# One transformer layer with an expert mixture: gate products of 256 columns in two parts, and 36 early expert blocks

## What is computed

```python
eid = jnp.take_along_axis(cand_i, pos, axis=-1)     # expert number: row * 128 + column
gate = jax.nn.softmax(top_s, axis=-1)
a = jnp.einsum('td,tkd->tk', hb, peer_u[eb], preferred_element_type=jnp.float32)
a = jax.nn.gelu(a, approximate=False)
return jnp.einsum('tk,tkd->td', (gb * a).astype(hb.dtype), peer_v[eb])
```

## Time and profile before

| | |
|---|---|
| median of the runs | 980.63 us (979.21 to 981.70) |
| the profiled execution | 980.77 us, span 979.0 us |
| TensorE busy | 962.2 us, 98% of the span |
| VectorE, ScalarE, GpSimd busy | 749.8, 464.6, 189.0 us |
| granted TensorE clock | 1.00 |
| gate stage, first to last product of L1788 | 246.3 to 324.4 us |
| moved | 172.57 MB |

### The profile page before, as it was taken

One profiled execution on the slowest core, in us unless ns is written; L12 is line 12 of the kernel. 1 busy time (PEld: TensorE's weight loads), 2 busy tenths in 40 slices (PEclk: granted clock), 3 DMA queues, 4 the chain that ended last, 5 costly groups with the idle time before them and its releaser, 6 DMA issues.

```text
span 979.0 us, 16833 instructions
## 1 busy us (share of the span) xinstructions
PE 962.2 (98%) x5606; PEld 845.1 (86%) x5606; DVE 749.8 (77%) x1385; ACT 464.6 (47%) x715; POOL 189.0 (19%) x232
## 2 busy tenths in 40 slices
PE   7999999999999999999999999999999999999998
PEld 7998899998999888888888888888888888888887
DVE  5899767988999887777777777777777777777776
ACT  5566544432777534444444444444444443444442
POOL 3064227986887100000000000000000000000000
PEclk9999999999999999999999999999999999999999
DMA  8633129845222676555555545555555555555554
GB/s 247 189 118 130 56 86 331 211 110 150 82 76 66 212 239 227 173 201 184 187 198 178 208 173 201 184 189 196 177 209 173 203 181 192 193 182 204 173 205 158
DMA packets 70164, 172.57 MB, mean 176 GB/s; under 512 B 6752, under 2 KB 35552, under 8 KB 69616
## 3 DMA queue, kind: packets, MB, share of 16 engines
q1 hardware_dynamic: 68080, 167.47, 50.7%
q0 software_dynamic: 576, 4.19, 2.1%
q10 hardware_dynamic: 1472, 0.44, 0.2%
HBM read 163.16 MB, written 4.72 MB: 171 GB/s over the span
## 4 chain that ended last, share of the span: by engine, by line
PE 75%; DVE 1%; issue 0%; POOL 0%; DVEq 0%
PE psum L1849 36%; PE psum L1829 20%; PE psum L1832 10%; PE psum L1788 6%; PE psum L1795 2%; PE psum L1715 1%; DVE big L1127 0%; PE psum L1478 0%; DVE big L1271 0%; DVE big L1138 0%; PE psum L1776 0%; DVE big L1173 0%; POOL big L1374 0%; DVE big L1169 0%; DVE big L1158 0%
## 5 line engine op out<-in xcount | busy, mean ns | idle before, releaser
L1849 PE MATMUL psum<-rr 128*128 128x512 f32 x1536 | 368.8, 391 | 0.0
L1849 PEld LDWEIGHTS psum<-rr 128*128 128x128 f32 x1536 | 287.9, 188 | 58.8
L1829 PE MATMUL psum<-h_all,rr 128*128 128x512 f32 x856 | 306.7, 392 | 0.0
L755 ACT ACTIVATE rr<-raw 128x1024 fp32r<-128x1024 f32 x109 | 115.6, 1060 | 274.5 <-PE psum L1849 274.5
L1193 DVE TENSOR_TENSOR rr<-raw,rr 128x1024 fp32r<-128x1024 f32 x109 | 133.6, 1225 | 145.6 <-ACT rr L755 145.6
L1832 PE MATMUL psum<-h_all,rr 128*128 128x256 f32 x856 | 221.9, 280 | 0.0
L1829 PEld LDWEIGHTS psum<-h_all,rr 128*128 128x128 f32 x856 | 160.6, 188 | 32.2 <-DVE rr L1132 0.6
L1832 PEld LDWEIGHTS psum<-h_all,rr 128*128 128x128 f32 x856 | 160.8, 188 | 8.3
L641 ACT ACTIVATE rr<-raw 128x1024 fp32r<-128x1024 f32 x107 | 113.6, 1061 | 61.9 <-DMA raw<-in_peer_u_dram 60.5
L1132 DVE TENSOR_TENSOR rr<-raw,rr 128x1024 fp32r<-128x1024 f32 x107 | 130.6, 1220 | 3.5 <-ACT rr L641 1.7
L1179 DVE TENSOR_TENSOR rr<-psum,picks 128x2048 fp32r<-128x2048 f32 x32 | 72.1, 2287 | 8.3 <-PE psum L1788 6.6
(11 more groups left out here) (202 smaller groups left out, 945.5 us busy)
## 6 DMA issues: line engine op xcount, KB each, us to landing
raw<-in_peer_u_dram SPq DMA_DIRECT2D x128, 512.0 KB, 4.0
raw<-in_peer_v_dram SPq DMA_DIRECT2D x128, 512.0 KB, 3.5
big<-in_w_in_dram SPq DMA_DIRECT2D x10, 1024.0 KB, 5.9
big<-in_peer_wq_dram SPq DMA_DIRECT2D x8, 1024.0 KB, 6.2
big<-in_w_out_dram SPq DMA_DIRECT2D x4, 1024.0 KB, 5.2
rr<-big POOLq DMA_DIRECT2D x4, 1024.0 KB, 8.6
up_kept<-gel SPq DMA_DIRECT2D x20, 128.0 KB, 3.6
gel<-up_kept SPq DMA_DIRECT2D x20, 128.0 KB, 3.5
```

The source lines that it names most:

```text
L755: act.activation(v_sp[s][:, 0, :], v_raw[s], ACT.Copy).then_inc(v_hi, 1)
L1829: return pe.matmul(both, ut[s][:, 0, k, :], ht[:, :, k, :], start=(k == 0), stop=(k == DK - 1))
L1849: i = pe.matmul(psum[:, 4 + 2 * t + n, :], g_sp[:, s, x, t * P:(t + 1) * P], v_sp[s][:, y, n * 512:(n + 1) * 512], start=(first and m == 0 ...
```

## The change

- A weight is kept as a high part (fp32r, in the buffer `hm`) and a low part (`picks[:, 2]`). The scaled columns of a token become 2 x 128 columns, one-hot x high and one-hot x low (`pairs_at`), fp32r. One fp32r product of 256 columns a token takes the place of the native one of 128 columns.
- A group's products go in two halves of four tokens, each into two PSUM banks. ScalarE copies the high half into `gates` (`keep_high`), VectorE adds the low half from PSUM (`add_low`).
- VectorE compares rows as before (1024 elements, iota in PSUM), and columns in bfloat16 with all operands in SBUF (`iota16`, `col16`), laid out [column][token], so that a token's columns lie 16 bytes apart. ScalarE scales three tokens of a group (six instructions of 128), GpSimd five (two of 640).
- 36 early blocks instead of 20, all native. TensorE's parts of blocks 13 to 35 are spread over the groups (`fill`): 12 parts ahead of the first group, 6 after the last, the other 166 between. They use the PSUM banks 0, 6 and 7 in turn. The Gelu of a block stands two groups behind its last part.
- `t32s` gets an SBUF buffer of its own, and so do the up weights of block 36 (`u_first`), which are loaded and split ahead of the gate stage.
- The values of blocks 0 and 1 are loaded while the last early blocks run, 2 and 3 after the last columns are scaled. `RING_END` is 31.

```diff
-NQ, OHS = SEQ // GRP, 3
-EARLY, EARLY_TOP = 20, 14
-RING_END = 19
-ACT_T = 2
+NQ, RS = SEQ // GRP, 3
+HALF = GRP // 2
+EARLY, EARLY_TOP = 36, 14
+RING_END = 31
+ACT_T = 3
+FILL0 = EARLY_TOP - 1
+PRE, TAIL = 12, 6
+def fill_end(q):
+    between = DK * (EARLY - FILL0) - PRE - TAIL
+    return PRE + (0 if q < 0 else between * (q + 1) // (NQ - 1) if q < NQ - 1 else between + TAIL)
+def filled_after(e):
+    return next(q for q in range(-1, NQ) if fill_end(q) >= DK * (e - FILL0 + 1))
...
+        cols = raw[:, 2 * D:3 * D].bitcast(BF16).rearrange("p (s n q) -> p s q n", s=2, q=GRP)
+        rows_at = [rr[:, n:n + D].rearrange("p (q n) -> p q n", q=GRP) for n in (2 * D, 3 * D, 6 * D)]
+        pairs_at = [rr[:, n:n + 2 * D].rearrange("p (q a n) -> p q a n", q=GRP, a=2) for n in (7 * D, 4 * D)]
+        def half_sums(c, part):
+            return psum[:, 2 + 2 * (c % 2):4 + 2 * (c % 2), :].rearrange("p b (q a n) -> p a n (b q)", q=2, a=2)[:, part]
         def early_bank(e):
-            return (2, 5)[e % 2] if e < EARLY_TOP - 1 else 0
+            return (2, 5)[e % 2] if e < FILL0 else (0, 6, 7)[(e - FILL0) % 3]
...
             def keep_early(e):
                 sp.wait_ge(e_up, e + 1)
-                if e + 3 < EARLY_TOP:
+                if e + 3 < EARLY:
                     load_ring(e + 3)
-                elif e < EARLY_TOP and e % 3 < 2:
-                    load_u(U_FIRST[e % 3])
-                elif e == EARLY - 1:
+                elif e == EARLY - 3:
                     sp.dma_start(v_first, pv[0]).then_inc(ld_vf, 16)
-                elif e >= EARLY_TOP:
-                    load_u(e + 2)
+                elif e == EARLY - 2:
+                    load_v(1)
+                if e == FILL0 - 4:
+                    sp.dma_start(u_first.rearrange("p k n -> p (k n)"), pu[EARLY]).then_inc(ld_uf, 16)
...
-            for b in range(1, 3):
-                sp.wait_ge(b_done, NQ - 3 + b)
+            sp.wait_ge(ohg_up, NQ)
+            sp.wait_ge(ohp_up, NQ)
+            for b in range(2, 4):
                 load_v(b)
...
-            act.activation(iota_in, iota, ACT.Copy).then_inc(a_iota, 1)
+            act.activation(iota_in, iota, ACT.Copy)
+            act.activation(iota16, iota.unsqueeze(2).to_broadcast([P, NK, GRP]), ACT.Copy).then_inc(a_iota, 1)
+            act.wait_ge(ld_uf, 16)
+            act.activation(ut[0][:, 0], u_first, ACT.Copy).then_inc(ut_hi, 1)
             act.wait_ge(d_sub, 1)
...
+            def gated(q, first, last):
+                for j in range(first, last):
+                    tok = GRP * q + j
+                    for part, scale in ((0, f(p_hi(tok, 1))), (1, picks[:, 2, tok:tok + 1])):
...
+                        i = act.activation(pairs_at[q % 2][:, j, part, :], cols[:, q % 2, j, :], ACT.Copy, scale=scale)
...
+            def keep_high(c):
+                act.wait_ge(b_done, c + 1)
+                act.activation(gates[:, :, HALF * c:HALF * c + HALF], half_sums(c, 0), ACT.Copy).then_inc(b_ev, 1)
             for q in range(NQ):
+                act.wait_ge(oh_up, 2 * q + 2)
+                if q >= 2:
+                    act.wait_ge(b_done, 2 * q - 2)
+                gated(q, 0, 1)
                 if q:
+                    keep_high(2 * q - 2)
+                    keep_high(2 * q - 1)
+                gated(q, 1, ACT_T)
+                for e in range(FILL0, EARLY):
+                    if filled_after(e) + 2 == q:
+                        early_gelu(e)
...
+            keep_high(2 * NQ - 2)
+            keep_high(2 * NQ - 1)
+            for e in range(FILL0, EARLY):
+                if filled_after(e) + 2 >= NQ:
+                    early_gelu(e)
...
+            def add_low(c):
+                dve.wait_ge(b_ev, c + 1)
+                mine = gates[:, :, HALF * c:HALF * c + HALF]
+                dve.tensor_tensor(mine, half_sums(c, 1), mine, ALU.add).then_inc(g_add, 1)
+            dve.wait_ge(ut_hi, 1)
+            dve.tensor_tensor(ut[0][:, 1], u_first, f(ut[0][:, 0]), ALU.subtract).then_inc(ut_lo, 1)
             for q in range(NQ):
+                if q >= RS:
+                    dve.wait_ge(b_done, 2 * (q - RS + 1))
+                ones(rows_at[q % RS], 0, GRP * q, GRP)
...
+                if q >= 2:
+                    add_low(2 * q - 4)
+                    add_low(2 * q - 3)
+                    dve.wait_ge(ohg_up, q - 1)
+                    dve.wait_ge(ohp_up, q - 1)
+                dve.tensor_tensor(cols[:, q % 2].rearrange("p q n -> p n q"), iota16, col16[:, GRP * q:GRP * q + GRP].unsqueeze(1).to_broadcast([P, NK, GRP]),
+                                  ALU.is_equal).then_inc(oh_up, 1)
...
+            def gated(q):
+                n, tok = GRP - ACT_T, GRP * q + ACT_T
+                for part, p in ((0, f(p_hi(tok, n))), (1, picks[:, 2, tok:tok + n])):
...
+                    i = pool.tensor_tensor(pairs_at[q % 2][:, ACT_T:, part, :], cols[:, q % 2, ACT_T:, :],
+                                           p.unsqueeze(2).to_broadcast([P, n, NK]), ALU.mult)
+                i.then_inc(ohp_up, 1)
             for q in range(NQ):
+                pool.wait_ge(oh_up, 2 * q + 2)
+                if q >= 2:
+                    pool.wait_ge(b_done, 2 * q - 2)
+                gated(q)
...
             def early_ready(e):
+                if e >= FILL0 + 3:
+                    pe.wait_ge(e_gel, e - 2)
...
+            def gate_half(q, h):
+                c = 2 * q + h
+                if c >= 2:
+                    pe.wait_ge(g_add, c - 1)
+                for j in range(HALF):
+                    i = pe.matmul(psum[:, 2 + 2 * (c % 2) + j // 2, (j % 2) * SEQ:(j % 2 + 1) * SEQ], rows_at[q % RS][:, HALF * h + j, :],
+                                  pairs_at[q % 2][:, HALF * h + j].rearrange("p a n -> p (a n)"), start=True, stop=True)
+                i.then_inc(b_done, 1)
...
+            early_part(EARLY_TOP - 2, DK // 2, DK).then_inc(e_up, 1)
+            fill(0, fill_end(-1))
+            pe.wait_ge(e_gel, EARLY_TOP - 1)
+            for q in range(NQ):
+                pe.wait_ge(ohg_up, q + 1)
+                pe.wait_ge(ohp_up, q + 1)
+                gate_half(q, 0)
+                gate_half(q, 1)
+                fill(fill_end(q - 1), fill_end(q))
...
+            pe.wait_ge(e_gel, EARLY - (EARLY - 1 - FILL0) % 3)
+            first_up(0, EARLY)
+            pe.wait_ge(g_add, 2 * NQ)
+            pe.wait_ge(e_gel, EARLY)
```

More of the change, by code:

```diff
@@ L118, in layer @@
         gel = sb("gel", [P, 2, SEQ])
+        t32s = sb("t32s", [P, DK, SEQ])[:, :, :]
+        u_first = sb("u_first", [P, DK, P])[:, :, :]
         psum = ctx.enter_context(nc.psum_tensor("psum", [P, 8, 512], F32))
@@ L212, in layer @@
         u_raw = raw[:, 0:2 * D].rearrange("p (s k n) -> p s k n", s=2, k=DK)
-        u_ring = [raw[:, n:n + D] for n in (0, D, 4 * D)]
+        u_ring = [raw[:, n:n + D] for n in ((D, 4 * D, 0)[(e - EARLY) % 3] for e in range(3))]
         v_raw = [raw[:, 2 * D:3 * D], raw[:, 4 * D:5 * D]]
@@ L706, in _ @@
             early_gelu(EARLY_TOP - 2)
[L708 to L716, removed]
-            act.wait_ge(pk_ev, 2)
@@ L720, in early_hi @@
[L720 to L727, removed]
-            for q in range(NQ):
[L730 to L737, removed]
-                if q:
[L739 to L749, removed]
@@ new lines, in gated @@
+            def gated(q, first, last):
+                for j in range(first, last):
+                    tok = GRP * q + j
+                    for part, scale in ((0, f(p_hi(tok, 1))), (1, picks[:, 2, tok:tok + 1])):
+                        if tok == 0 and part:
+                            act.wait_ge(d_plo, 1)
+                        i = act.activation(pairs_at[q % 2][:, j, part, :], cols[:, q % 2, j, :], ACT.Copy, scale=scale)
+                if last == ACT_T:
+                    i.then_inc(ohg_up, 1)
@@ new lines, in fill @@
+            def fill(first, last):
+                for n in range(first, last):
+                    e, k = FILL0 + n // DK, n % DK
+                    if k == 0:
+                        early_ready(e)
+                    i = early_part(e, k, k + 1)
+                    if k == DK - 1:
+                        i.then_inc(e_up, 1)
+            early_part(EARLY_TOP - 2, DK // 2, DK).then_inc(e_up, 1)
+            fill(0, fill_end(-1))
+            pe.wait_ge(e_gel, EARLY_TOP - 1)
+            for q in range(NQ):
@@ L1783, in gate_group @@
                 pe.wait_ge(ohg_up, q + 1)
                 pe.wait_ge(ohp_up, q + 1)
-                if not first:
-                    pe.wait_ge(b_ev, q - OHS + 1)
-                for j in range(GRP):
-                    i = pe.matmul(psum[:, 2 + 2 * s + j // 4, (j % 4) * P:(j % 4 + 1) * P], f(oh[:, s, 0, j, :]), oh_g[:, s, j, :],
-                                  start=True, stop=True)
-                i.then_inc(b_done, 1)
-            def split_part(e, first, last):
-                for k in range(first, last):
```

(4 more changed lines are left out.)

92 lines of the change are left out of this document (29 added, 63 removed).

## The result

The changed kernel takes 983.00 us (980.75 to 983.96), the kernel before in the same comparison 980.75 (978.90 to 981.98): a ratio of 1.0026, 95% interval 1.0016 to 1.0035. So the forecast gain of 11 us is not there. The kernel stands 2.3 us above the one before: the interval leaves out 1, but that is less than the 2.9 us that the prediction took as the least it could tell. The profiled execution took 983.88 us, its span 982.1.

The account below looks back on a forecast made before the run. TensorE was taken to bound the kernel nearly everywhere. 980.8 - 11.9 (TensorE net) + 0.3 (start) + 0.5 (downs) = 969.7 us against the profiled execution, 969.5 against the median; range 965 to 990.

Parts of the forecast that it names:

- The pace of the stage: Gate stage: TensorE slowest at 3.26 us a group, against VectorE 3.1, ScalarE 3.0 and GpSimd up to 3.2.
- I take no surcharge: Gate stage: ScalarE's and GpSimd's reads of 16-bit columns at a 16-byte step were charged nothing extra.
- A row that speaks against the change: Passage on strided column reads: VectorE's L1127 at 64 bytes needs 1.90 ns an element, against 1.18 for neighbours.
- the 0.72 that I had as the upper end: Gate stage: highest surcharge considered for the 16-byte step, in ns an element, from VectorE's strided row.
- Rival 1: Gate stage: ScalarE sets the pace, deciding from 0.345 us a copy; 973 to 981 us, chance 0.25.
- rival 2: Gate stage: GpSimd sets the pace, products 1.59 us, round 3.87; 989 us, slower than before, chance 0.2.
- the lead of 0.2 us of TensorE: Gate stage: TensorE at 3.26 us a group is slowest by 0.2, a narrow lead and most of the risk.
- The lock: Gate stage: VectorE's column comparison, both operands in SBUF, holds GpSimd up, making its round 3.2 us.
- TensorE's prices: TensorE: native part 0.432 us, gate product 0.1185, late block's up product 2.77; net change -11.9 us.
- The wait ahead of the first down product: After the gate stage: store and load, 3.6 us each, leave TensorE idle 4.1 us; ends nothing and 4.5.
- The start and the downs: Ahead of the gate stage, u_first's load and copy add 0.3 us; late value loads in down blocks add 0.5.
- the half microsecond of cover: Before the gate stage: about half a microsecond spare around u_first's copy; without it up to 0.7 us more.

Follow-up runs that it names:

- the first two runs: Changed kernel with neighbouring elements in place of the 16-byte step, for ScalarE alone (982.30 us), then for GpSimd alone (981.38 us).
- the second run: Changed kernel with GpSimd reading neighbouring elements and ScalarE keeping its 16-byte step: 981.38 us, ratio 1.0006.

## Why the prediction was wrong

The forecast went down by 11.1 us against the profiled execution, and the span went up by 3.1. By its steps:

**The pace of the stage: the step that failed.** It is "I take no surcharge" for the 16 bytes, under "A row that speaks against the change". For ScalarE no reason was given; for GpSimd it was that GpSimd's 1.92 ns an element is already as slow as the strided read of L1127. One slow rate did not hide the other: read at 16 bytes GpSimd took 1.574 / 640 = 2.46 ns. ScalarE's copies went from 0.30 to 0.42 or 0.43 from start to start, 0.94 to 1.02 ns an element more, above the 0.72 that I had as the upper end. The stage is 31 x (3.73 - 3.26) = 14.6 us longer than forecast, and with both readers on neighbours the time fell from 983.00 to 967.25. The row that mattered was there; it was put in a rival instead of in the sum.

**The two rivals, taken as alternatives.** Rival 1 wanted 0.345 us a copy and rival 2 1.29 us a product; 0.42 and 1.574 passed both. I gave them 0.25 and 0.2 as separate cases, though both hang on the same layout. Had the step been dear for one engine alone, the time would still have been about 982, as the first two runs show, so the lead of 0.2 us of TensorE was even less safe than I wrote. The price of rival 2 came out (1.59 against 1.574), but by luck: it was the rate of a product with two full operands (L1452), and with the step gone the same product took 1.257. Its sum did not come out: 3.87 a group counted the full duration of both products, while the second starts 0.05 before the first ends, and 0.06 for the comparison; 3.73 was measured.

The Trainium skill ("GPSIMD Engine Reference", section 7, "Performance pitfalls for Q7 kernels") puts the price of a read at a step over 8 bytes at half as much again, and names 8 bytes as the edge. The edge agrees with these runs, none at 8 and a price at 16; the size was smaller than stated, 25% on the whole instruction (1.257 to 1.574).

**The lock.** I let the comparison hold up GpSimd. In the stage it is the other way: the comparison, 0.68 us alone, lasted 1.02 in the median because it started while a product ran (where GpSimd was fast, in the second run, it had 0.681 on the mean), and GpSimd then waited 0.63 for it. Thirty such waits and 7.0 ahead of the first product are the 25.9 us of idle time on the page. The 0.63 in the round was right by luck: it was meant as the length of the comparison, and what came is its last 0.55 and 0.08 to GpSimd's start.

**TensorE's prices** held. The 16 parts ahead of the first group took 6.91 us, as forecast, and the run with both engines on neighbours shows the pace of 3.263. The late blocks still follow each other after 5.52 us (484.85 to 490.37 in the chain). The chain that ended last has these pieces in the changed kernel (start, duration):

```profile
242.30 6.91 PE psum L1743 x32
...
366.82 2.61 DMA up_kept<-gel
...
369.44 2.00 DMA gel<-up_kept
...
372.00 4.55 DMA gel<-up_kept
```

**The wait ahead of the first down product** is 1.6 us instead of 4.1: the store took 2.61 and the load 2.00, where I had 3.6 for each from a store and a load in other company. That gives back 2.5 us. The load for the third block, last in the rows above, was slower (4.55) and is the first of the late loads below.

**The start and the downs.** The transposes ended 1.04 us later than before (242.30 against 241.26) and not 0.3; the delay lies ahead of every new instruction of the mixture, at a wait for the transfers of the low parts (1.4 us at the longest, 0.7 before). In the other runs that wait's longest was 0.5 to 1.2, and their transposes ended between 240.90 and 242.91. So the 1.04 lies within the spread from run to run; with one trace of the kernel before, it is not shown whether a part of it is the change's own. In four of the experiments the chain there runs over the u_first load (5.5 to 6.1 us to landing), so there the half microsecond of cover in the prediction was used up. From the first down product on, the span is 42.5 us shorter (609.2 against 651.7) where the forecast had 43.8. The last three waits of the list above, 0.4 to 0.6 us each, are late loads there and come to 1.4 instead of 0.5; the other 0.4 is not accounted for.

Sum: -11.1 + 0.7 (start) + 14.6 (pace) - 2.5 (wait) + 1.3 (downs) = +3.0, against +3.1 measured in the span. So the gain on TensorE was there; the readers of the 16-bit columns took it back in the stage.

## What to carry to other kernels

A layout that makes one engine's instruction cheap sets the price of all its readers: before taking it, give each reader's step its own surcharge, from the dearest strided row in the trace rather than from none. Where two engines share such a cause, they are one case and not two, and relieving one shows almost nothing in the time: relieve both, or shrink the step (here 8 bytes instead of 16) before drawing a conclusion. Work that is moved to the bounding engine in such a stage is free only as long as another engine is slower there; count the round of each engine per group, and fill up to the slowest.

## What the runs showed of the hardware that was not expected

ScalarE too pays for a step of 16 bytes between 16-bit elements: 0.397 us for 128 neighbours, 0.411 at 8 bytes, 0.538 at 16. The prediction had no row for that engine. The Trainium skill ("SBUF — State Buffer", section "Specifications (TRN2)") has lines of 16 bytes that want two hits each for the full rate. The three durations agree with it: two of these elements lie in a line at 8 bytes, one at 16.

Eight comparisons of 128 elements with a scalar took 1.38 us against 0.68 for one of 1024 with two tensors, on 16-bit operands: at this size eight starts cost more than one instruction. And with 20 early blocks TensorE, busy 23.2 us of 40 in the stage and waiting in every group, showed a granted clock of 0.81 there, with stretches at 0.50 in which eight gate products took 2.08 us instead of 1.22; in the same stretch of the changed kernel it was busy 37.5 of 40, at 1.00.
